# A reordered start, gate rows stored from another queue, and adaLN tiles loaded one chunk later in a macaron block kernel

## What is computed

```python
cond = silu(c)
mod = cond @ w_ada + b_ada
sh1, sc1, gt1, sh2, sc2, gt2, sh3, sc3, gt3 = split(mod, 9)
u = rmsnorm(h, norm1_g) * (1 + sc1) + sh1
a, b = split(u @ ffn1_w_in, 2)              # 2048 -> 2 x 5632
h = h + 0.5 * gt1 * ((silu(a) * b) @ ffn1_w_out)
u = rmsnorm(h, norm2_g) * (1 + sc2) + sh2
h = h + gt2 * mixer(u)                      # w_in (proj, rest, gates), w_att_up, w_mlstm_up, w_out
u = rmsnorm(h, norm3_g) * (1 + sc3) + sh3
h = h + 0.5 * gt3 * swiglu(u, ffn2_w_in, ffn2_w_out)
return rmsnorm(h, final_g)
```

## Time and profile before

| | |
|---|---|
| median of 3 runs | 2039.84 us (2038.3 to 2039.84) |
| profiled execution, as a run | 2043.58 us |
| its span, first to last instruction | 2041.8 us |
| TensorE busy | 2019.9 us, 99% |
| VectorE busy | 1685.4 us, 83% |
| ScalarE busy | 1206.6 us, 59% |
| DMA | 544.96 MB, mean 267 GB/s |
| mean granted TensorE clock | 0.997 |

### The profile page before, as it was taken

The page is one execution under the profiler, slowest core; times in us unless marked ns, Lnnn a source line. Parts: engine busy times, 40 slices in busy tenths (PEclk is TensorE's granted clock), DMA queues, the critical chain, the costliest instruction groups (busy, mean ns, idle before and its releaser), DMA issues.

```text
span 2041.8 us, 23814 instructions
## 1 busy us (share of the span) xinstructions
PE 2019.9 (99%) x9090; PEld 1662.6 (81%) x9090; DVE 1685.4 (83%) x2208; ACT 1206.6 (59%) x1658; POOL 2.4 (0%) x14
## 2 busy tenths in 40 slices
PE   8999999999999999999999999999999999999998
PEld 6788888887888888888777888888888888888887
DVE  7898698878889988788998898887777777787786
ACT  5777644655345555446555676567775577755764
POOL 0000000000000000000000000000000000000000
PEclk8999999999999999999999999999999999999999
DMA  9998799899999868976665687575565556555554
GB/s 386 393 380 310 286 346 385 329 310 372 364 357 345 311 244 347 343 278 182 221 219 209 237 304 270 184 234 179 206 229 204 192 179 210 209 199 201 173 198 150
DMA packets 102658, 544.96 MB, mean 267 GB/s; under 512 B 17424, under 2 KB 19728, under 8 KB 53776
## 3 DMA queue, kind: packets, MB, share of 16 engines
q1 hardware_dynamic: 101696, 543.30, 73.1%
q10 hardware_dynamic: 848, 0.14, 0.0%
HBM read 541.28 MB, written 2.12 MB: 266 GB/s over the span
## 4 chain that ended last, share of the span: by engine, by line
PE 93%; DMA 3%; DVE 2%; ACT 1%; issue 1%; SPq 0%; DVEq 0%; ACTq 0%
PE pa L934 13%; PE pb L934 13%; PE pa L942 13%; PE pb L942 12%; PE pb L938 12%; PE pa L938 12%; DMA raw<-in_ffn_w_in_dram 2%; PE pa L1028 2%; PE pa L1034 2%; PE pa L1031 2%; DMA raw<-in_w_first_dram 1%; PE pa L949 1%; PE pq L1201 1%; PE pa L1192 1%; PE pb L1201 1%; PE pa L1197 1%
## 5 line engine op out<-in xcount | busy, mean ns | idle before, releaser
L1452 ACT CAST hi<-raw 128x1024 fp32r<-128x1024 f32 (+2 forms) x662 | 679.1, 1034 | 694.9 <-PE pa L942 251.5
L2040 DVE TENSOR_TENSOR lo<-raw,hi 128x1024 fp32r<-128x1024 f32 (+2 forms) x662 | 784.6, 1201 | 277.3 <-ACT hi L1452 274.3
L2057 DVE SCALAR_TENSOR_TENSOR ada_w<-ada_w,cond_row 128x1024 f32<-128x1024 f32 x207 | 247.2, 1218 | 0.0
L934 PE MATMUL pa<-hi,act_hi 128*128 128x512 f32 x800 | 222.0, 393 | 0.0
L934 PE MATMUL pb<-hi,act_hi 128*128 128x512 f32 x800 | 217.1, 393 | 0.1
L942 PE MATMUL pb<-lo,act_hi 128*128 128x512 f32 x800 | 213.9, 389 | 0.0
L942 PE MATMUL pa<-lo,act_hi 128*128 128x512 f32 x784 | 213.6, 389 | 0.0
L938 PE MATMUL pb<-hi,act_lo 128*128 128x512 f32 x784 | 209.8, 389 | 0.0
L938 PE MATMUL pa<-hi,act_lo 128*128 128x512 f32 x720 | 196.0, 389 | 0.0
L942 PEld LDWEIGHTS pb<-lo,act_hi 128*128 128x128 f32 x800 | 150.2, 188 | 31.4
L934 PEld LDWEIGHTS pb<-hi,act_hi 128*128 128x128 f32 x800 | 148.6, 188 | 32.4 <-issue 2.2
(11 more groups left out here) (462 smaller groups left out, 2612.5 us busy)
## 6 DMA issues: line engine op xcount, KB each, us to landing
raw<-in_ffn_w_in_dram SPq DMA_DIRECT2D x107, 1024.0 KB, 5.1
ada_w<-in_w_ada_dram SPq DMA_DIRECT2D x207, 512.0 KB, 6.5
raw<-in_ffn_w_out_dram SPq DMA_DIRECT2D x60, 1024.0 KB, 6.8
raw<-in_w_first_dram SPq DMA_DIRECT2D x48, 1024.0 KB, 6.9
raw<-in_w_gates_dram SPq DMA_DIRECT2D x32, 1024.0 KB, 4.9
raw<-in_w_proj_dram SPq DMA_DIRECT2D x31, 1024.0 KB, 5.7
pair<-in_ffn_w_in_dram SPq DMA_DIRECT2D x20, 1024.0 KB, 6.9
raw<-in_ffn_w_out_dram SPq DMA_DIRECT2D x24, 768.0 KB, 4.6
```

Source lines behind the costliest of these rows:

```text
L934: pe.matmul(bank[:, tt, cols], a_hi[:, k0 + kk, tok], w_hi[:, kk, cols], start=start and kk == 0, stop=False, skip_group_check=on)
L1452: act.copy(hi_of(ph, i, j, half)[:, 0:n, 0:w], raw_of(ph, i, j)[:, 2 * half:2 * half + n, 0:w])\
L2040: dve.tensor_tensor(lo_of(ph, i, j)[:, s, 0:w], raw_of(ph, i, j)[:, s, 0:w], hi_of(ph, i, j, half)[:, 0:n, 0:w].bitcast(F32), ALU.subtract)\
L2057: dve.scalar_tensor_tensor(out=wt, in0=wt, scalar=1.0, in1=cond_row[:, half * ADA_W:(half + 1) * ADA_W], op0=ALU.mult, op1=ALU.mult, accum ...
```

## The change

STAGES: stage 0 takes kt 0 for pair 0 alone, stage 1 takes kt 0 and then kt 1 for pair 1, and pair 0 takes its kt 1 later, together with 2 and 3. Start tiles 2 and up are used two units later, and loaded up to a chunk later. The moves of stage 0 stand behind the cast of unit last + 1. The three gate stores are issued by ScalarE: GT1's in the last group of ffn1_in1 at step 8, GT2's in rest at step 5, GT3's in the first group of ffn2_in0 at step 8. The 512 KB tiles planned before proj are issued by SyncE behind the load of the next chunk.

```diff
--- before.py
+++ after.py
@@ -48,8 +48,8 @@
 
 
 GROUPS = 6
-STAGES = [(0, ((0,), (1,))), (1, ((0, 1),)), (2, ((0, 1),)),
-          (2, ((2,), (3,))), (1, ((2, 3),)), (0, ((2, 3),)),
+STAGES = [(0, ((0,),)), (1, ((0,), (1,))), (2, ((0, 1),)),
+          (2, ((2,), (3,))), (1, ((2, 3),)), (0, ((1, 2, 3),)),
           (0, ((4,), (5, 6))), (1, ((4, 5, 6),)), (2, ((4, 5, 6),)),
           (2, ((7,), (8, 9), (10, 11))), (1, ((7, 8, 9, 10, 11),)), (0, ((7, 8, 9, 10, 11),))]
 LEFT = range(12, 16)
@@ -176,10 +176,11 @@
     assert t == len(TILES), t
     gates_tiles = [t for cidx in tiles_at for t in tiles_at[cidx] if 0 <= cidx - plan["gates"].c0 < 32]
     AHEAD = 2
+    LATER = 1
     load_at = {}
     for cidx in sorted(tiles_at):
         for t in tiles_at[cidx]:
-            load_at.setdefault(cidx + (AHEAD if t in gates_tiles else 0), []).append(t)
+            load_at.setdefault(cidx + (AHEAD if t in gates_tiles else LATER if cidx < plan["proj"].c0 else 0), []).append(t)
     ring_of = {}
     for ring in (gates_tiles, [t for t in range(len(TILES)) if t not in gates_tiles]):
         size = 2 if ring is gates_tiles else ADA_RING
@@ -213,11 +214,11 @@
 
     def tile_unit(k):
 
-        return (0, 0, 1, 2)[k] if k < 4 else 3 + round(2.2 * (k - 4))
+        return (0, 0, 2, 4)[k] if k < 4 else 5 + round(2.2 * (k - 4))
 
     def load_before(k):
 
-        return k // 2 if k < 4 else tile_unit(k) // 2 + 1
+        return (0, 0, 1, 2)[k] if k < 4 else tile_unit(k) // 2 + 1
 
     def hi_unit(kt):
 
@@ -674,12 +675,6 @@
                     sp.wait_ge(s_dve, k - S_RING + 1)
                 sp.dma_start(start_home(k), w_ada[m * KD + kt, :, :]).then_inc(ada_s_in[k % S_RING], 16)
 
-            def store_gate(m, done):
-
-                sp.wait_ge(mod_ok, mod_count(m))
-                sp.dma_start(gate_rows[ROWS_OUT.index(m):ROWS_OUT.index(m) + 1, :].rearrange("a (k p) -> p (a k)", p=P),
-                             mod[:, m * KD:(m + 1) * KD], allow_slow_non_contiguous=True).then_inc(done, 16)
-
             def load_gate(row, done, landed):
 
                 sp.wait_ge(done, 16)
@@ -785,13 +780,9 @@
                             load_ada(plan[name].at(i) + j)
                             if name == "ffn1_in2" and (i, j) in ((1, 4), (1, 7)):
                                 load_x_again(2 + (j == 7))
-                            if (name, i, j) == ("ffn1_in1", 3, 3):
-                                store_gate(GT1, gt1_out)
                             if (name, i, j) == ("ffn2_in0", 0, 4):
                                 load_pair(0, 0)
                                 load_pair(0, 1)
-                            if (name, i, j) == ("ffn2_in0", 0, 7):
-                                store_gate(GT3, gt3_out)
                     over(sp, ng, ffn_in)
                     name = f"ffn{f}_out{p}"
                     def ffn_out(b, first, name=name, g0=g0, ng=ng):
@@ -827,7 +818,6 @@
                 over(sp, 4, body)
 
             proj_pair("proj", w_proj)
-            store_gate(GT2, gt2_out)
             for j in range(4):
                 load(plan["rest"], 0, j, w_rest[:, j * 4:j * 4 + 4, :], 4, REST_W)
             proj_pair("gates", w_gates)
@@ -1723,7 +1713,7 @@
 
                 todo = {}
                 for k, move in enumerate(MOVES):
-                    todo.setdefault(move[0] + 3, []).append(k)
+                    todo.setdefault(move[0] + (1 if move[1] == 0 else 3), []).append(k)
                 assert [k for u in sorted(todo) for k in todo[u]] == list(range(len(MOVES)))
                 for u in range(N_UNITS):
                     split(ph, 0, u // 2, u % 2, 2)
@@ -1775,6 +1765,17 @@
                     silu(ph)(i)
                     nat_evac_at(nb - 1, i - 1)
 
+            def store_gate(m, done):
+
+                act.wait_ge(mod_ok, mod_count(m))
+                act.dma_start(gate_rows[ROWS_OUT.index(m):ROWS_OUT.index(m) + 1, :].rearrange("a (k p) -> p (a k)", p=P),
+                              mod[:, m * KD:(m + 1) * KD], allow_slow_non_contiguous=True).then_inc(done, 16)
+
+            def first_gate(n_):
+
+                if n_ == 8:
+                    store_gate(GT1, gt1_out)
+
             def rows_load(k):
 
                 if k == 0:
@@ -1802,6 +1803,8 @@
 
             def first_casts(n_):
 
+                if n_ == 8:
+                    store_gate(GT3, gt3_out)
                 if n_ == 10:
                     s_casts("ffn2_in0")
                 if n_ >= 12:
@@ -1820,6 +1823,7 @@
                             continue
                         in_body(ph, i, i == 0, silu(ph), None, True, mid=mid if p == 0 else None,
                                 step=rows_load if (f, p, i) == (1, 2, 0) else
+                                first_gate if (f, p, i) == (1, 1, 3) else
                                 first_casts if (f, p, i) == (2, 0, 0) else None)
                         if (f, p, i) == (1, 2, 2):
 
@@ -1885,6 +1889,8 @@
                     act.activation(m_st[:, 8:10, :], m_st[:, 10:12, :], ACT.Ln, bias=1.0).then_inc(g_ln, 1)
                 if n_ == 3:
                     copy_b(3)
+                if n_ == 5:
+                    store_gate(GT2, gt2_out)
 
             def qk_silu(hds):
```

## The result

| | median, us | lowest to highest | ratio to before, 95% interval |
|---|---|---|---|
| before | 2039.84 (4 runs) | 2038.30 to 2039.84 | |
| after | 2049.33 (4 runs) | 2048.67 to 2050.97 | 1.0049 [1.0033, 1.0065] |

The change made the kernel slower by 0.49%, some 10 us, where 8 us less were forecast; the time lies outside the range. The profiled execution of after has a span of 2047.0 us and 2048.72 as a run.

What follows compares the result with a forecast made beforehand. TensorE, busy 99% of the span, was taken as the bound, losing time in four places. Gains of 3.1 (start) + 4.9 (stores) + 0 (late tiles) = 8.0 us gave 2039.8 - 8.0 = 2031.8 us, range 2029.5 to 2037.0.

Steps and rivals of the forecast that it cites:

- Part 1, the start: New start order: 4.3 us gained at full clock, 1.2 of it at 80 us; 3.1 after the clock term (1.4 to 4.9).
- if the clock stays up: At the start: seventh unit at 39.1 instead of 42.17, 3.1 us gained provided the clock does not fall.
- The term for the clock: At the start: a clock fall after the new 2.1 us idle stretch, taken to cost 1.2 us.
- Part 2, the stores: Gate stores on ScalarE's queue: 4.9 us gained (0 to 5), 3.4 at 485 and 1.5 at 1379.
- At some 75 a us 2048 pieces take 27 us, spread out: GT1 store on ScalarE's queue: pieces leave slowly beside the weights, instead of about 5 us in a heap.
- So I expect no outage: Behind the moved stores: weights keep flowing, so the 3.4 us at 485 and 1.5 at 1379 go.
- the first rival: Stores' 4-byte writes stop the other queue as well; outage moves 13 us later, costs the same: 2036.7 us; chance 0.17.
- At the GT2 store no wait of TensorE is found: GT2 store in the profile before: no TensorE wait seen; no gain or loss was put on moving it.
- GT1's load back: SyncE's load at about 465 to 468, store landing 464 to 470; blocking there: net 2055 us, chance 0.05.
- Part 3, late tiles: adaLN tiles one chunk later: VectorE waits about 1 us per such tile; 0 net, bounds +0.5 and -3.
- Once it is 1 us behind, the tiles are in time: VectorE, three units (some 7 us) ahead of TensorE, absorbs the late tiles' wait; cost 0.
- the second rival: In out1 and in2 VectorE waits for late tiles and TensorE sees it: 1 to 3 us back, about 2034; chance 0.12.

Runs made afterwards that it cites:

- e1: Kernel before with only the three gate stores issued by ScalarE at the places of the change; 2048.48 us, ratio 1.0046.
- e2: Kernel before with only the new order of the start (stages, start tiles, moves of stage 0); 2036.61 us, ratio 0.9989.
- e12: Kernel before with only the gate rows turned on VectorE and stored as 16 pieces of 512 bytes; 2036.65 us, ratio 0.9984.
- e9: Kernel before with new start, gate rows turned (16 pieces of 512 bytes, SyncE's queue) and late tiles; 2034.47 us, ratio 0.9973.
- e5: Changed kernel with only GT2's store back on SyncE's queue behind the proj loads; 2039.99 us, ratio 1.0005.
- e6: Kernel before with only GT2's store moved behind the four w_rest loads, still on SyncE's queue; 2047.35 us, ratio 1.004.
- e11: Kernel before with only GT2's store on ScalarE's queue at an early place, issued at 904.0; 2040.04 us, ratio 1.0.
- e3: Kernel before with only the 512 KB tiles of the first FFN loaded one chunk later; 2041.81 us, ratio 1.0016.
- e7: Changed kernel with all three stores back on SyncE's queue at their old places; 2039.62 us, ratio 1.0004.
- e10: Changed kernel with gate rows turned on VectorE and stored as 16 pieces of 512 bytes from ScalarE's queue; 2034.79 us, ratio 0.9974.
- e8: Kernel before with new start and gate rows turned, 16 pieces of 512 bytes on SyncE's queue, no late tiles; 2034.99 us, ratio 0.9978.

## Why the prediction was wrong, step by step

**Part 1, the start: right in its steps, near in its sum by luck.** The third unit came 0.6 us later than forecast, the fifth 0.7, the seventh 0.6. The first unit began 0.6 us later than in the profile of before already (20.12 against 19.48); counted from it, the steps fit to 0.1 us. What failed is what they were held against. The 3.1 us "if the clock stays up" set a start at full clock against 42.17, from an execution whose clock was down. e1 has the old start with the clock up, its first and seventh unit here:

```profile
20.01 0.70 PE L1182 MATMUL pa<-hi,act_hi 128*128 128x512 f32 x2 [0.39 <-ACT act_hi L1699]
...
40.21 1.07 PE L1182 MATMUL px<-hi,act_hi 128*128 128x512 f32 x4
```

That is 20.2 us, and after takes 19.6: at full clock the order gains 0.6 us there, not 3.1. At 80 us 0.87 were lost in place of 1.86, 1.0 us gained where 1.2 were forecast. Together 1.6 us, not 4.3. The rest of what e2 shows is the clock. From the first to the 61st unit the six profiles with the old start take 169.0 to 171.5 us, on average 170.1, and the eight with the new one 167.4 to 168.6, on average 168.0. This agrees with the 2.2 us of e2 (0.4 to 4.1), whose interval has the forecast of 3.1 in it.

The term for the clock had no basis either: the fall of the earlier trace rows is not a property of the code. The stretch from 25 to 38 in e1 and e12, both with the old start, and in e9 with the new one:

```profile
25.00:38.00 13.00, 10.37 (x43) 7.73 (x44) 12.29 (x17) 7.76 (x9) 0.00 (x0) 1.00 1.01 427
```

```profile
25.00:38.00 13.00, 10.52 (x40) 8.28 (x40) 12.29 (x17) 8.25 (x10) 0.00 (x0) 0.87 1.01 428
```

```profile
25.00:38.00 13.00, 10.83 (x40) 8.03 (x39) 10.07 (x12) 7.97 (x9) 0.00 (x0) 0.87 1.02 425
```

The old start had 0.74, 0.87 and 1.00, the new one 1.00 and 0.87. The idle stretch before the fall, or before none, was 2.49 us in e1 (no fall) and 2.48 in e12, 1.92 in after (no fall) and in e9. Whether such a stretch is followed by a fall differs from one execution to the next.

**Part 2, the stores: the failed step.** "At some 75 a us 2048 pieces take 27 us, spread out" and, from it, "So I expect no outage" were wrong. On ScalarE's queue 1855 pieces left in 2 us, over ten times that rate, and the hole came with them. It is there whichever queue they were on: 96 GB/s over 8 us here, and in the kernel before, by the same view, 45 GB/s from 433 to 441. The row that the rate was taken from did not carry it. Its 189 packets in 2 us are 94 a us and not 75, and they belong to loads (pos_i, sink_row, gb_row; only 27 of them have 4 bytes), not to a store. The 16.0 us to landing, read as the pace at which the store of before drained, has the hole in it: there too 1833 small packets left from 431 to 433. The landing after about 27 us did come (27.5), but by luck: e1, with the same store on the same queue at 435.9, has 13.6, e5 has 25.9, and in after 71 last pieces trickled out up to 461.6.

That is the first rival in its mechanism, given 0.17. The rule of the Trainium skill quoted for it (DMA: Bandwidth & Descriptors, "Issuing engines are not separate DMA queues") agrees with e6 beside the changed kernel, 8.2 us and 9.0 us lost on the one queue and the other. What the Trainium skill says of turns by packets ("Queues, rings and completion order" on the same page) is not seen here as one packet for one, 1855 against 94 in 2 us; whether it counts packets as the profile does, no run shows.

The rival's price failed as well, and this is most of the loss. It had the outage "costs the same", and the sentence "At the GT2 store no wait of TensorE is found" was taken as a licence to move that store at no cost. That store had a hole all the same, and no wait because of what lay behind it. At 936 there lie the first chunks of 1 MB of w_gates, and a gate_w tile on which VectorE's series in front of the softmax depends. A hole of the same kind costs 8.2 to 9.4 us there (e6, e5 against after, e1). No rival carried this: of the moved transfers only GT1's load back was checked, whose wait did not come (the store landed at 461.9, the load was issued at 468.56 and took 0.43 us).

Of the 4.9 us forecast, the 3.4 at GT1 stayed. The 1.5 at GT3 did come: after, e1 and e5 have no wait of TensorE there. But the hole is there too (64 GB/s from 1367 to 1373 in after), so it was not for the reason given; no run moved that store alone. The gain may also have been over-read. Removing all three holes for good, which the change did not do, brings 3.3 us (e12), and in 420 to 520 the profile of before lost 3.6 us where e2, e11 and e6 lost 1.5 to 2.7. That profiled execution was a long one: 2043.58 us as a run, while before's own runs in the experiments had medians of 2038.9 to 2040.1 and none above 2041.97. The interval of e12 reaches to 5.1, so 4.9 is not excluded.

**Part 3, late tiles: mis-sized.** Forecast 0, bounds +0.5 and -3; measured 3.3 us lost (e3, 1.6 to 5.1), and 3.1 between e7 and e2. "Once it is 1 us behind, the tiles are in time" holds only without a hole (e9). In the hole VectorE now waits up to 4.4 us (5.7 in e3) for a tile that before had already been in its slot, and the splits behind it come late: 1.3 to 3.5 us more on TensorE from 420 to 520. This is the second rival (1 to 3 us, 0.12) in the first FFN's out1, with the hole as its condition, which had been left out because Part 2 had removed it. The two steps were summed as if independent, and the second leaned on the first.

**The sum as measured:** -2.2 (start) + 3.3 (late tiles beside a hole) + 9.0 (GT2's store) + about 0 (GT1 and GT3) = 10.1, against 10.0.

**What stays open.** Why the chip is slow for some 8 to 9 us behind 2048 writes of 4 bytes. The traces show that it begins as the pieces leave and that pieces of 64 and 512 bytes do not cause it, not where the writes queue up. Nothing between 4 and 64 bytes was tried, nor fewer pieces of 4. Open too are why TensorE's wait at GT3 went, what sets the landing of such a store, and what decides whether the clock falls at the start.

## What to carry to other kernels

Here a DMA that writes 2048 pieces of 4 bytes slows the loads behind it to a fraction for 8 to 9 us, whether SyncE or ScalarE issues it. Look at which loads lie in the 15 us behind its issue, and move it only to where these have slack. Better, remove the pieces: four 32 x 32 transposes of 0.2 us each turned 2048 pieces into 16 and gained 3.3 us in a kernel at 99% TensorE. Hold a forecast of a start against several executions, not one whose clock happened to be low. A wait that the profile does not show is no proof that the place of a transfer is free; and a cover that one step of a change relies on must be priced for the case that the other step fails.

## What the runs showed of the hardware

- 2048 writes of 4 bytes leave in a heap on either queue: 1855 in 2 us on ScalarE's (after, 438 to 440), about 1833 in 2 us on SyncE's (before, 431 to 433). Behind them all queues together move 96 and 45 GB/s over 8 us, and over 6 us behind other such stores 55 (after), 16 (before) and 66 GB/s (e6). With 128 pieces of 64 bytes the stretches at 936 and 942 move 324 and 244 GB/s.
- The landing of such a store on ScalarE's queue took 27.5, 25.9 and 13.6 us at nearly the same place (after, e5, e1), and 14.9 at 936. 16 pieces of 512 bytes took 3.0 to 5.1 us there (e10) and 4.6 to 8.1 on SyncE's queue (e8, e9, e12).
- The granted clock after idle stretches of 1.9 to 2.8 us differed between executions of the same start (0.74, 0.87, 1.00 as the mean of 25 to 38). During a wait of 4.9 us, behind one of 1.45, it fell to its lower level.
